# Second feed-forward product by seven block products instead of eight, in twelve of the fourteen passes of a four-layer transformer kernel

## The reference

```python
# A: width 4096
u = _rms(x, norm2) @ w_ff1
x = x + jnp.square(jax.nn.relu(u)) @ w_ff2
# B: width 2816; h is the output of the first layer norm
up = h @ ffn_w_up                      # 1024 x 5632: a half to be convolved, a half that multiplies
g = gelu(causal_conv3(up_a) + bias) * up_b
x = layer_norm(alpha * h + g @ ffn_w_down)
```

## Time and profile before

| | |
|---|---|
| runs | 2916.51, 2921.14, 2924.66 us |
| profiled execution, span | 2923.6 us (the profile's own time; nothing else is given around it) |
| granted TensorE clock, mean | 0.969 |
| POOL, whole span | 170.2 us (6%) |
| weight transfers | 212 MB read, 20.2% of 16 DMA engines |

### The profile page before, as it was taken

The page is one execution under the profiler, slowest core; times in us unless marked ns, Lnnn a source line. Parts: engine busy times, 40 slices in busy tenths (PEclk is TensorE's granted clock), DMA queues, the critical chain, the costliest instruction groups (busy, mean ns, idle before and its releaser), DMA issues.

```text
span 2923.6 us, 45193 instructions
## 1 busy us (share of the span) xinstructions
PE 2783.6 (95%) x20028; PEld 2299.7 (79%) x20028; DVE 1440.3 (49%) x2242; ACT 988.4 (34%) x1490; POOL 170.2 (6%) x166
## 2 busy tenths in 40 slices
PE   8989999999989999999999799999999897999998
PEld 7877888878768888887768778888887587788887
DVE  4575533344475444433454574343634645743436
ACT  4344322233344232323342233232333522332422
POOL 0200000001100000000013300000000033000000
PEclk9998999999989999999989899999999898999999
DMA  5102222223003222221000033222220001132221
GB/s 192 50 1 97 87 101 96 92 73 114 17 8 136 94 94 101 93 92 52 15 1 30 20 128 115 90 102 90 85 73 29 1 3 46 73 130 101 87 101 58
DMA packets 31011, 216.83 MB, mean 74 GB/s; under 512 B 3680, under 2 KB 3936, under 8 KB 6368
## 3 DMA queue, kind: packets, MB, share of 16 engines
q1 hardware_dynamic: 30816, 213.94, 20.2%
HBM read 211.83 MB, written 2.10 MB: 73 GB/s over the span
## 4 chain that ended last, share of the span: by engine, by line
PE 88%; DVE 8%; ACT 2%; issue 1%; PEld 0%; PEldq 0%; DMA 0%; ACTq 0%; SPq 0%; DVEq 0%
PE PS L570 81%; PE PS L573 3%; PE PS L771 2%; DVE SC L1381 2%; DVE X L1389 1%; DVE R L1381 1%; DVE SM L1392 1%; PE PS L1185 1%; PE PS L1135 1%; DVE LN L1381 0%; PE PS L855 0%; DVE SM L1381 0%; ACT LN L2172 0%; PE PS L764 0%; PEld PS L570 0%
## 5 line engine op out<-in xcount | busy, mean ns | idle before, releaser
L570 PE MATMUL PS<-H,SPL 128*128 128x512 f32 (+1 forms) x4560 | 1054.2, 391 | 5.5 <-DVE H L1389 4.0
L570 PEld LDWEIGHTS PS<-H,SPL 128*128 128x128 f32 (+1 forms) x4560 | 851.5, 188 | 188.5 <-issue 7.0
L1381 DVE TENSOR_TENSOR SPL<-RAW,SPL 128x2048 fp32r<-128x2048 f32 (+3 forms) x192 | 429.6, 2239 | 680.5 <-ACT SPL L2172 677.5
L2172 ACT ACTIVATE SPL<-RAW 128x2048 fp32r<-128x2048 f32 (+3 forms) x192 | 358.0, 1868 | 783.0 <-PE PS L570 754.8
L570 PE MATMUL PS<-SPL,Uu 128*128 128x512 f32 x2592 | 589.8, 389 | 0.0
L570 PEld LDWEIGHTS PS<-SPL,Uu 128*128 128x128 f32 x2592 | 486.5, 188 | 101.0
L570 PE MATMUL PS<-SPL,H 128*128 128x512 f32 (+2 forms) x2016 | 432.1, 375 | 2.3 <-DVE SPL L1381 1.6
L570 PEld LDWEIGHTS PS<-SPL,H 128*128 128x128 f32 x2016 | 363.7, 189 | 69.2 <-DVE SPL L1381 2.1
L2172 ACT ACTIVATE R<-PS 128x512 f32<-128x512 f32 (+1 forms) x154 | 88.5, 584 | 187.0 <-PE PS L570 156.3
L1381 DVE TENSOR_TENSOR R<-R,PS 128x512 f32<-128x512 f32 (+1 forms) x98 | 64.8, 661 | 106.6 <-PE PS L570 91.2
L2172 ACT ACTIVATE Uu<-R 128x512 fp32r<-128x512 f32 x108 | 68.3, 632 | 142.2 <-DVE R L1381 142.2
(11 more groups left out here) (240 smaller groups left out, 2481.7 us busy)
## 6 DMA issues: line engine op xcount, KB each, us to landing
RAW<-in_wA SPq DMA_DIRECT2D x84, 1024.0 KB, 4.8
RAW<-in_wB SPq DMA_DIRECT2D x84, 1024.0 KB, 4.8
RAW<-in_wAo SPq DMA_DIRECT2D x8, 1024.0 KB, 4.8
RAW<-in_wBo SPq DMA_DIRECT2D x8, 1024.0 KB, 5.0
LN<-in_ln SPq DMA_DIRECT2D x4, 1024.0 KB, 6.6
P<-in_pB SPq DMA_DIRECT2D x2, 1920.0 KB, 9.1
RAW<-in_wBm SPq DMA_DIRECT2D x4, 704.0 KB, 4.0
X<-in_x SPq DMA_DIRECT2D x4, 512.0 KB, 5.6
```

Source lines behind the costliest of these rows:

```text
L570: return pe.matmul(out, l_, r_, start=start, stop=stop)
L1381: return v.tensor_tensor(out, a, b, o)
L2172: return a.activation(out, in_, f, scale=scale)
```

## The change

In twelve passes (all four of each A layer, the first two of each B layer; `QUADS`) the down product is done as a 2 x 2 block product by seven block products and sums instead of eight block products. The hidden operand is cut in two by tokens (EARLY, LATE: 256 each) and in two by features (512 each): A11 (late tokens), A21 (early tokens) of the first features, A12 and A22 of the others. The four weight groups are B11, B21, B12, B22. Each product is one group of 24 matmuls (2 banks x 4 k x 3):

| order | left | right | | order | left | right |
|---|---|---|---|---|---|---|
| P1 | A11 | B11 | | P7 | S3 = A11-A21 | T3 = B22-B12 |
| P2 | A12 | B21 | | P5 | S1 = A21+A22 | T1 = B22-T2 |
| P6 | S2 = A22-S3 | T2 = B11+T3 | | P3 | S4 = A12-S2 | B22 |
| P4 | A22 | T4 = T2-B21 | | | | |

The weight sums T3, T2, T4, T1 (128 x 2048) and the operand sums S2, S1, S4 (128 x 1024) are made by POOL, S3 by DVE. There are four raw buffers (two of RAW, the new RW2, and LN), and seven pairs of high and low parts a pass instead of four. P6 goes on in the banks of P1, P7 in those of P6, and P3 in those of P5, each after DVE has added the bank's earlier state to x (16 additions a pass instead of 8). In A the square is now made from PSUM by DVE (max with 0, times the row factor RB spread by four matmuls) and ACT (Square), and x gets a plain addition.

```diff
+PRODUCTS = ("P1", "P2", "P6", "P4", "P7", "P5", "P3")
+FACTORS = ("B11", "B21", "T2", "T4", "T3", "T1", "B22")
...
+        raw_slots = [RAW[:, 0:2048], RAW[:, 2048:4096], RW2[:, 0:2048], LN[:, 0:2048]]
...
+            def quad(key):                                    # PE
+                base, ready = n["xadd"], n.get("ul", 0)
+                added_to = {("P6", 0): 1, ("P6", 1): 2, ("P7", 0): 5, ("P7", 1): 6, ("P3", 0): 13, ("P3", 1): 14}
+                for name in PRODUCTS:
...
+                    pe.wait_ge(s.lo, i + 1)
+                    pe.wait_ge(s.ul, ready + lows)
...
+                low_parts()                                   # DVE, quad
+                low_operand("A12", slice(2, 4))
+                add("P1", 0, 2, 0, True)
+                add("P1", 1, 3, 0, True)
+                low_operand("S2")
+                low_parts()
+                add("P2", 0, 2, 0)
+                add("P2", 1, 3, 0)
+                low_operand("A22")
+                low_parts()
+                add("P6", 0, 2, 1, True)
+                add("P6", 1, 3, 1, True)
+                low_operand("S1")
+                low_parts()
...
                 for p in range(4):                            # DVE, A layers
-                    for q in range(2):
-                        chunk(2)
-                        for b in range(4):
...
-                            tt(T, T, T, ALU.mult).then_inc(s.fv, 1)
-                            v.wait_ge(s.uh, n("uh"))
-                            tt(u2(i)[1], T, u2(i)[0].bitcast(f32), ALU.subtract).then_inc(s.ul, 1)
+                    def squared(q, b):
+                        v.wait_ge(s.mm, full_at[(l, "up", p, q), b])
+                        stt(RU[q][:, b], bank(sets[q][b]), 0.0, RB, ALU.max, ALU.mult).then_inc(s.fv, 1)
...
+                    low_parts()
+                    low_parts()
+                    v.wait_ge(s.rc, l + 1)
+                    for b in range(4):
+                        squared(0, b)
+                    low_parts()
+                    low_operand("A11")
+                    difference()
+                    low_parts()
+                    low_operand("S3")
+                    for b in range(3):
+                        squared(1, b)
+                    low_operand("A12", slice(0, 2))
+                    squared(1, 3)
...
+                high_operand("A12", slice(2, 4))              # ACT, quad
+                high_parts()
+                a.wait_ge(s.gs, n("gs"))
+                high_operand("S2")
+                high_parts()
+                high_operand("A22")
...
+                high_parts()
...
+            def quad(l, p):                                   # POOL
...
+                g.wait_ge(s.raw[held["B12"]], landed["B12"])
+                g.wait_ge(s.raw[held["B22"]], landed["B22"])
+                weight_sum("T3", B["B12"], B["B22"], B["B12"], ALU.subtract)
+                g.wait_ge(s.lo, j + 1)
+                g.wait_ge(s.tw, sums + 1)
+                weight_sum("T2", B["B11"], B["B11"], B["B12"], ALU.add)
+                g.wait_ge(s.lo, j + 2)
+                g.wait_ge(s.tw, sums + 2)
+                weight_sum("T4", B["B21"], B["B11"], B["B21"], ALU.subtract)
+                g.wait_ge(s.uh, highs + 4)
+                g.wait_ge(s.ul, lows + 2)
+                tt(S2, A22, S3, ALU.subtract).then_inc(s.gs, 1)
...
+                g.wait_ge(s.lo, j + 3)
+                g.wait_ge(s.tw, sums + 3)
+                weight_sum("T1", B["B11"], B["B22"], B["B11"], ALU.subtract)
+                tt(S1, A21, A22, ALU.add).then_inc(s.gs, 1)
...
+                g.wait_ge(s.ul, lows + 3)
+                g.wait_ge(s.gs, n["gs"] - 1)
+                tt(S4, A12, S2, ALU.subtract).then_inc(s.gs, 1)
```

More of the change, by code:

```diff
@@ L1321, in tensor @@
                     for q in range(2):
[L1322 to L1329, removed]
+                        chunk((l, "up", p, q), 2, of_h2, "F", sets[q], freed=lambda b: (s.fv, n("fv")),
+                              between=(lambda: spread_roots(l)) if p == q == 0 else None)
+                    quad((l, "down", p))
             for l in range(2):
@@ L1440, in chunk, with paid, low_operand @@
                             evict(b)
+            def paid():
+                while at["owed"]:
+                    at["owed"] -= 1
+                    low_parts()
+            def low_operand(which, ks=slice(0, 4)):
+                i, a_ = OPERANDS[which]
+                hi, lo = operand(i)
+                v.wait_ge(s.uh, n("uh"))
+                ins = tt(four(lo)[:, ks], a_[:, ks], four(hi)[:, ks].bitcast(f32), ALU.subtract)
+                if ks.stop == 4:
+                    ins.then_inc(s.ul, 1)
+                    n("ul")
@@ L2047, in post @@
                 yield
+            last_sum = {}
             v.wait_ge(s.psm, 16)
@@ L2659, in scalar, with squared @@
                 for p in range(4):
[L2660 to L2671, removed]
+                    def squared(q, b):
+                        a.wait_ge(s.fv, n("fv"))
+                        act(RU[q][:, b], RU[q][:, b], ACT.Square).then_inc(s.fg, 1)
+                        n("fg")
+                    paid()
+                    high_parts()
+                    if p == 0:
+                        a.wait_ge(s.gtr, 2 * l + 2)
+                        act(RB, bank(4), ACT.Copy).then_inc(s.rc, 1)
+                    high_parts()
+                    for b in range(4):
+                        squared(0, b)
+                    a.wait_ge(s.fg, n["fg"])
+                    high_operand("A11")
+                    high_parts()
+                    a.wait_ge(s.us, n("us"))
+                    high_operand("S3")
+                    high_parts()
+                    squared(1, 0)
+                    squared(1, 1)
+                    a.wait_ge(s.fg, n["fg"])
+                    high_operand("A12", slice(0, 2))
+                    squared(1, 2)
+                    squared(1, 3)
+                    a.wait_ge(s.fg, n["fg"])
+                    left = quad((l, "down", p), "rms" if p == 3 and l == 0 else None)
             for l in range(2):
@@ L2910, in sync @@
             sp.dma_start(PSM[:, 0:NPS], ap["psm"]).then_inc(s.psm, 16)
-            for i, (src, w) in enumerate(stream):
+            for i, (l_, k_, where, landed, freed) in enumerate(loads):
+                src, w = stream[first_load(l_) + k_]
                 if i == 3:
```

389 lines of the change are left out of this document (342 added, 47 removed).

## The result

The changed kernel takes 2953.88 us (median of 4 runs, 2945.56 to 2955.36) against 2921.58 for the kernel before on the same chip: a ratio of 1.0098, 95% interval 1.0076 to 1.0119. Its profiled execution has a span of 2953.6 us, 30.0 more than before. It is slower, as forecast, but by about half of the forecast: 2987 had been said, +66 us; the medians give +32, the ratio +29, the spans +30.

What follows compares the result with a forecast made beforehand. PE's matmuls were taken to bound the kernel. A passes +34.3, B passes +24.8, clock 5 and row factor 2 gave +66 us on the profile's 2923.6, 2990; the median, 2.5 below the span, 2987; range 2915 to 3020.

Steps and rivals of the forecast that it cites:

- T3 on the convolution step: Second B pass: POOL's T3 also collides with a DVE convolution step (4.6 us), making P2 9.1 us late.
- the exclusion costs little: Rival: POOL's sums slip between DVE's; only gaps of 1.8 (A) and 1.3 us (B) stay: 2877 us, chance 0.14.
- DVE keeps the turn: Rival: DVE's next ready instruction goes first, S3 before T2; A pass 89.6 to 90.6, total 2960 to 2972 us, chance 0.2.
- the forecast's own 2970 to 3005: Main case: exclusion in full with turns, including the ends for clock and POOL's 2048 row; 2970 to 3005 us, chance 0.42.
- steps 2 to 4: A pass, up to P2: POOL's T2, T4 and S2 hold back DVE's S3 and low parts; P2 gap 6.4 us.
- the prediction's clock: Time scale of the forecast pass: 0 is the start of its first up group; P1 at 43.6 in A.
- step 5: A pass, behind P2: POOL's T1, S1, S4 alternate with DVE's low parts; P6 0.45 us late, P4 2.87.
- The 5 us for the clock: Half clock after P2's gaps, 0 to 16 us in all; 5 taken.
- The prediction's own alternative: Half clock for 3.2 us behind P2's start costs P2 1.6 us, covered by P4's wait of 2.9: nothing added.
- the B passes, +24.8 forecast: POOL's sums also delay convolution steps; P2 7.7 and 9.1 us late, passes +5.5 and +6.9, twice: +24.8 us.
- The row factor and everything outside the passes: Row factor's four matmuls, about 1 us in each A layer: +2; code and data in new buffers: 0.

Runs made afterwards that it cites:

- narrow: Changed kernel with POOL's four weight sums done on only 64 of 2048 columns: 2896.40 us, ratio 0.9918 to the kernel before.
- dve_sums: Changed kernel with all sums but T3 on DVE, and A12's second-half low part ahead of T2's: 2862.97 us, ratio 0.9803 to the kernel before.
- filler: Changed kernel with twenty unneeded matmuls between P1 and P2 in each of the twelve passes: 2964.14 us, ratio 1.0141 to the kernel before.
- only_a: Changed kernel with seven products in the A layers alone, B layers as before the change: 2937.00 us, ratio 1.0042 to the kernel before.
- swap: Changed kernel with DVE making the low part of A12's second half ahead of T2's: 2954.85 us, ratio 1.0114 to the kernel before.
- dve_order: dve_sums with the changed kernel's DVE order, T2's low part ahead of A12's second half: 2883.24 us, ratio 0.9855 to the kernel before.
- weight_sums_dve: dve_sums with S2, S1 and S4 left on POOL: 2908.62 us, ratio 0.9953 to the kernel before.

## Why the prediction was right in direction and wrong in size

**Right: the mechanism.** POOL's sums and DVE's instructions with two SBUF inputs exclude each other whole, in the places named but one (T3 on the convolution step, which came in one layer of two). Shortening POOL's instructions (narrow) or moving them (dve_sums) turned the loss into a gain. The rival that the exclusion costs little is out: narrow and dve_sums are what it would have looked like. The rival "DVE keeps the turn" has the nearer numbers (89.6 to 90.6 said for a pass, 89.1 measured; 2960 to 2972 in all, 2954 measured; the forecast's own 2970 to 3005 does not hold the result), but its mechanism is not there: with S3 next in DVE's list, POOL's T2 was let in between low A11 and S3.

**Wrong: the size of P2's gap (steps 2 to 4), 4.94 us where 6.4 had been forecast.** On the prediction's clock (up group at 299.8 in the trace) low B11 ends at 28.6 as forecast. T2 ends at 34.2 (34.6 forecast), S3 at 35.3 (35.8), low S3 at 41.7 (42.4), T4 at 46.2 (47.1), low A12's first half at 46.7 (47.8), the last bank at 47.3 (48.5), low T2 at 53.3 (54.6), low A12's second half at 53.8 (55.3). The 1.5 us came from many small steps of one kind. POOL's duration is right: 4.61 us in the row below, where nothing holds it back, against the 4.67 taken.

```profile
1830.19 4.61 POOL L3184 TENSOR_TENSOR RAW<-RAW 128x2048 f32<-128x2048 f32 x1 [14.39 <-DVE SPL L1555]
```

But an instruction that has waited is finished sooner than its recorded duration after the one that held it: T2 ended 4.45 us after low A11 (329.58 to 334.03), T4 4.49 after low S3, S3 1.09 after T2 instead of 1.22. On one engine the next instruction starts about 0.08 us before the recorded end of the one before it (326.15 + 2.29 = 328.44, the next at 328.36). The prediction had added up full durations, with 0.05 for a hop between engines, and should have taken about 0.1 off at each such place, 0.2 behind a blocked instruction. The Trainium skill ("GPSIMD Engine Reference", Elementwise — side-by-side cycle accounting) gives 4497 ns for this instruction; the trace agrees within 3% of 4.61, and closer with the 4.45 behind another engine's end.

**Wrong: step 5 and the clock, 2.4 us a pass where 3.3 and 5 us on top had been forecast.** The waits before P6 and P4 were to be 0.45 + 2.87 us. P4 came 13.25 us after P2 instead of 14.2, that is 2.4 us behind its matmuls. The kind of the term is right: the chain from low A12's end to low A22's was to take 14.2 us and took 13.26 (353.70 to 366.96), short by the same small steps as before P2. The 5 us for the clock were not there. The prediction's own alternative holds, that P2's loss at half clock is covered by P4's wait: in filler P4 comes at the same distance with the clock full. The loss (1.7 to 2.6 us) was larger than the 1.6 of that alternative, so that it just fills the wait; all that it added is 0.3 us in the first pass and some 0.6 in the twelve.

**Wrong: the B passes, +24.8 forecast, +11.3 by the lengths of their seven products.** P2 came 5.3, 5.3, 5.6 and 6.9 us late where 7.7 and 9.1 had been forecast, and P4's 2.4 stands in place of 3.3 here too. In the first pass (P1 at 1843.43, 87.1 on the prediction's clock) T2 started at 73.9 (75.0 forecast), T4 ended at 85.8 (87.3), the last multiplication at 91.9 (94.1) and low A12 at 97.8 (100.2). The convolution steps behind T4 lost 4.4 us (5.89 against 1.54 for the next such pair), nearly the 4.65 forecast. So about half of the 2.4 us was there before any collision: the low part of B11, which releases T2, came 1.2 us earlier than the prediction had it. The text of the prediction does not show how it placed that part, so the cause of this 1.2 us stays open. In the second pass the collision with T3 came in one layer of two.

In all, an A pass: forecast 81.65 + 6.4 + 3.3 = 91.4, measured 81.65 + 4.94 + 2.4 = 89.0. Of the 36 us too much the A passes are about 19, the clock term 5 and the B passes 13. That the result lies within 2915 to 3020 owes much to the width of that range.

**Right: the small things.** The row factor and everything outside the passes were put at +2; with the A passes at +2.0 each, 15.6 in all, only_a's +12 to +17 leaves room for no more than that. The row factor alone was not measured. The loads were in time for PE in all passes.

## What to carry to other kernels

Count an idle engine's time as free only after asking which instructions of the others it stops: here 10 us more of DVE a pass and POOL left to T3 is some 86 us faster than the "free" engine, with DVE's order changed as well. When a whole chain of an in-order engine is late, reordering it moved the gap (swap) and filling the gap moved the wait (filler); taking time out of the chain helped, and only then did the order count too (dve_order). A half clock behind a gap and an operand wait within the same stretch are one term: take the larger of the two, do not add them.

## What the runs showed of the hardware

- In these runs of dense matmuls the granted clock stayed at 1.00 (2.4 GHz) after PE gaps of 1.47, 1.53 and 1.71 us (4, 8 and 4 cases) and went to 0.50 (1.2 GHz) after all eight of 1.95 us and all of 4.4 to 6.7 us. Gaps of 2.00 to 2.06 us came out both ways: 0.50 after two of ten in filler and nine of twelve in weight_sums_dve, 1.00 after the others. The same gap in the same kernel can do either.
- The half clock behind a gap of about 2 us cost the product behind it 1.6 us, behind the gaps of 4.8 to 6.7 us 1.7 to 2.6 us; in the changed kernel an operand wait covered nearly all of that.
- POOL's 128 x 2048 f32 sum takes 4.61 us, DVE's 2.29: POOL is twice as slow, and each stops the other. An instruction that had waited for the other engine's end was over sooner after it than its free duration: 4.45 and 4.49 us for the first, 1.09 for DVE's 1.22.
- The turn goes to the engine that waits, whenever the other's instruction ends, even if its next one is ready: low A11, T2, S3 in the changed kernel, and S2, low A12, S1, low T2, S4 in weight_sums_dve.
